# A fused two-block transformer kernel on one core: the queries' RMS norm moved into the exponential's scale, the keys' sums of squares taken in two rounded parts

## The chip, the core and the metric

The kernel runs on one core of one Trainium2 chip, whatever else the chip has. The metric is device time in microseconds from start to end of the program. The core has a matrix engine (TensorE, PE in the profile, with its weight loads as PEld), a vector engine (VectorE, DVE), an activation engine (ScalarE, ACT), a general engine (GpSimd, POOL) and a queue engine (SyncE, SP) that issues the DMAs.

## The reference, cut to what matters

The first block (attention with compressed, selected and window branches, retention, a gated feed-forward part) is not touched. The second block has two layers; each projects the tokens, and its attention normalizes queries and keys before a softmax:

```python
q1 = rms_norm_2(q[..., 0, :], q_norm_g[i])      # over the 64 numbers of a half head
q2 = rms_norm_2(q[..., 1, :], q_norm_g[i])
k1 = rms_norm_2(k[..., 0, :], k_norm_g[i])
k2 = rms_norm_2(k[..., 1, :], k_norm_g[i])
def rms_norm_2(x, g):
    y = xf * lax.rsqrt(jnp.mean(xf * xf, axis=-1, keepdims=True) + EPS)
    return (y * g).astype(x.dtype)
s = einsum('bhqd,bhkd->bhqk', q, k) * 64 ** -0.5
att = softmax(mask(s1)) - lam * softmax(mask(s2))
```

There are 512 tokens, 4 heads of two halves of 64 numbers, and 2 such layers.

## The kernel before, in words

All activations lie turned: 128 features over the partitions, 512 tokens along the free dimension. Weights come in as a stream of units of 128x1024 numbers. For each unit ScalarE rounds the raw numbers to a high part (`hi_part`, called by `ahead`, line 396), GpSimd takes the rest in four quarters (`lo_part`, line 339), and TensorE makes 8 times three products of 512 columns in the one-pass type F32R: high by high, high by low, low by high (`product`, lines 745 to 747). A unit is 24 matmuls. The order of each engine's work is written out by hand; semaphores with running counts tie the engines together. The two-part operands of the tokens are `a_hi`, `a_lo` and `y_hi`, `y_lo`.

A layer of the second block begins with four units for the values, then eight units (`L_QK`) that give in turn the queries and the keys of a head: unit j even is the queries of head j/2, j odd the keys. While TensorE runs unit j, the other engines finish unit j-1:

- VectorE, `qk_in(j-1)`: multiplies the PSUM bank by the tokens' norm (`scaled`, line 1220), squares the result (line 1768) and tells TensorE.
- TensorE, ahead of the fourth of the 8 triples of unit j (`k == 3`): `square_sum` (line 780), a full fp32 matmul of 512 columns with `ones2`, a block matrix of ones that sums over each half head and leaves the sum on all its 64 rows.
- ScalarE, `ahead` first, then `tile_root` (lines 411 and 419): the square root of the 128x512 sums.
- VectorE one unit later, `qk_out(j-2)`: the reciprocal of 128x512 numbers (line 1774), and the product of tile, gain and reciprocal into `qn` or `kn` (line 1777).

Then come 16 mixing slots (`L_MIX`), of one unit each. The last two tiles of queries and keys are finished in slots 0 and 1. Between the slots lie the first 8 of the 16 attention steps of the layer, one for each head and each 128 queries: scores (line 1078), mask and maximum (`maxima`, lines 1394 to 1408), exponential with a bias per row and a constant scale (`softmax_step`, line 511), the division (`step_probs`, lines 1808 to 1813), transposes at `k == 5` of the odd slots (line 1090), and the product with the values (line 1102). Slots 2 to 5 also hold a matmul of the pooled tiles (line 1136) at `k == 6`; VectorE's `pooled_out` (1823, 1826) and `mix` (1842 to 1855) run beside them.

Of the kernel before, what the change touches and what calls it, by code (L numbers as in the profile page):

```python
# [24 lines left out]
F32R = mybir.dt.float32r  # L25
# [4 lines left out]
P = 128  # L30
# [113 lines left out]
def build(nc, stream, xT, tab, decay, rope, par1, par2, pT, out):  # L144
    ctx = ExitStack()
    with ctx:
        def sb(name, shape, dt=F32):
            return ctx.enter_context(nc.sbuf_tensor(name, shape, dt))

        def sem(name):  # L150
            return ctx.enter_context(nc.semaphore(name))
# [32 lines left out]
        mix_gain = sb("mix_gain", [P, LAYERS * KD])  # L184
        work = sb("work", [P, 9 * S + 288])

        ident = cst[:, K_ID:K_ID + P]
# [3 lines left out]
        tile_a, tile_b, tile_d = ta[:, 16:], tb[:, 16:], td[:, 16:]  # L191
        eps = small[:, 60:61]
        decay_t = h[:, 0:4, :]
        rope_cn, rope_sn, rope_cr, rope_sr = (h[:, 4 + i, :] for i in range(4))
# [34 lines left out]
        merge_bank = [b_r0, b_r1, bank[0], bank[1]]  # L229

        first_unit_landed = sem("first_unit_landed")
        landed = [sem("block_landed_0"), sem("block_landed_1")]
# [152 lines left out]
        def _(act):  # L385
# [156 lines left out]
            for t in range(RH):  # L542
                u0 = t * RET_UNITS + U_RET
                for j in range(RET_UNITS):
# [3 lines left out]
                                  (prob[:, 0, 0:n], b_s0[:, 0:n], 1),  # L548
                                  (prob[:, 1, 0:n], b_s1[:, 0:n], 2)], DH ** -0.5)
                    if j == 4 or j == 0 and t > 0:  # L550
# [83 lines left out]
            for layer in range(LAYERS):  # L634
# [12 lines left out]
                def attention_step(s):  # L647
                    n = (s % QT + 1) * P
                    softmax_step([(prob[:, e, 0:n], (b_s0, b_s1)[e][:, 0:n], e) for e in range(2)],
                                 64 ** -0.5)  # L650
# [18 lines left out]
                for k in range(16):  # L669
                    if k > 0 and k % 2 == 0:  # L670
                        attention_step(k // 2)
                    ahead(ul + L_MIX, k)
                    if k == 0:
                        tile_root(tile_c, b_r1[:, :], 1.0 / 64)
# [52 lines left out]
        def _(pe):  # L727
# [68 lines left out]
            def bank4(j):  # L796
                return bank[(j + 2) % 4][:, :]
# [261 lines left out]
            for layer in range(LAYERS):  # L1059
# [48 lines left out]
                for j in range(8):  # L1108
                    unit(ul + L_QK, j, 4, [bank4(j)], a_op(), 8,
                         lambda k, j=j: square_sum((b_r0, b_r1)[(j - 1) % 2], ones2, (tile_b, tile_c)[(j - 1) % 2])  # L1110
                         if k == 3 and j > 0 else None)
# [12 lines left out]
                def mixed(slot, k):  # L1124
# [6 lines left out]
                    if k == 3 and slot == 0:  # L1131
                        square_sum(b_r1, ones2, tile_c)
                    if k == 6 and 2 <= slot <= 5:
# [56 lines left out]
        def _(dve):  # L1190
# [90 lines left out]
            V.memset(ptc, 0.0).then_inc(vector_step, steps.up())  # L1281
            V.wait_ge(vector_step, steps.now())
            V.memset(eps_squared, EPS * EPS).then_inc(vector_step, steps.up())
            V.memset(eps, EPS).then_inc(to_activate, pre.up())
# [23 lines left out]

            V.wait_ge(constants_landed, 32)
            V.wait_ge(parameters_landed, 16)  # L1310

# [75 lines left out]

            def maxima(i, mask, scale, cmp=0):

# [13 lines left out]
                if cmp:  # L1403
# [3 lines left out]
                b = 2 + cmp  # L1407
                V.tensor_scalar(small[:, 0:b], small[:, 8:8 + b], -scale, None, ALU.mult)\
                    .then_inc(max_ready, mx.up())
                V.wait_ge(max_ready, mx.now())  # L1410
# [315 lines left out]
            for layer in range(LAYERS):  # L1726
# [35 lines left out]

                value, square = (tile_a, tile_d), (tile_b, tile_c)

                def qk_in(j):
                    x, sq = value[j % 2], square[j % 2]
                    scaled(x, bank4(j), ul + L_QK, j)
                    V.tensor_tensor(sq, x, x, ALU.mult).then_inc(squares_ready, sums.up())
                    V.wait_ge(squares_ready, sums.now())

                def qk_out(j):
                    x, root_tile = value[j % 2], square[j % 2]
                    V.wait_ge(root_ready, root.due())
                    V.reciprocal(root_tile, root_tile).then_inc(vector_step, steps.up())
                    V.wait_ge(vector_step, steps.now())
                    gq = (C2_QG, C2_KG)[j % 2]
                    ins = V.scalar_tensor_tensor(out=(qn, kn)[j % 2][:, j // 2, :], in0=x,
                                                 scalar=par[:, gq:gq + 1], in1=root_tile,
                                                 op0=ALU.mult, op1=ALU.mult)
                    if j % 2:  # L1780
                        ins.then_inc(retention_input_ready, rin.up())
                        V.wait_ge(retention_input_ready, rin.now())
                    else:
                        ins.then_inc(vector_step, steps.up())

# [16 lines left out]
                def step_maxima(s):  # L1802
                    maxima(s % QT, chunk, 64 ** -0.5)

# [447 lines left out]
```

## Time and profile before

| | |
|---|---|
| Runs of the kernel | 2649.3, 2649.35, 2649.73 us (median 2649.35) |
| The profiled execution's own time | 2649.99 us |
| Its span in the profile | 2648.2 us |
| TensorE busy | 2599.5 us, 98% |
| VectorE, ScalarE, GpSimd busy | 1576.3, 849.6, 1526.7 us (60%, 32%, 58%) |
| Chain that ended last, TensorE's share | 88% |

A row of a group tells how many instructions it has, their busy time and the mean of one. A row of the timeline gives start and length in us, the engine, the line of the kernel, output and inputs, and in brackets how long the engine was idle before it and who ended that. Two matmul rows overlap, since a matmul's record runs to its drained end: what it costs in a stream is the distance between the starts.

### The profile page before, as it was taken

How to read it: one execution, taken by the hardware profiler on the slowest of the kernel's cores; microseconds unless marked ns; L12 is line 12 of the kernel's file. 1: busy time of each engine (PE TensorE's matmuls, PEld its weight loads, DVE VectorE, ACT ScalarE, POOL GpSimd, SP SyncE). 2: the span in 40 equal slices, each digit the busy share in tenths (PEclk: the TensorE clock that was granted, in tenths of full speed). 3: DMA queues.
4: the chain of work that ended last, by engine and by line, in shares of the span. 5: the costliest groups of instructions: out<-in, count | busy, mean ns of one | idle time of the engine just before them, and what ended most of it. 6: DMA issues, size and time to landing. Idle time of an engine off the chain costs nothing.

```text
span 2648.2 us, 33256 instructions
## 1 busy us (share of the span) xinstructions
PE 2599.5 (98%) x11819; PEld 2086.0 (79%) x11819; DVE 1576.3 (60%) x2192; ACT 849.6 (32%) x1245; POOL 1526.7 (58%) x1820
## 2 busy tenths in 40 slices
PE   8999999999999998999999999999899999999999
PEld 6777777888888876777888888887677788888887
DVE  6666774388483767855575432657774448443275
ACT  5444444223222332354322111133235532111122
POOL 6634345566666753554666655764355456665576
PEclk9999999999999999999999999999999999999999
DMA  5311112222223221222223222232122222222223
GB/s 188 125 49 51 62 55 105 97 95 96 96 94 107 99 102 64 80 83 92 104 80 112 96 95 95 95 111 89 62 80 96 80 104 86 105 96 95 95 95 127
DMA packets 36832, 247.47 MB, mean 93 GB/s; under 512 B 4464, under 2 KB 4848, under 8 KB 7792
## 3 DMA queue, kind: packets, MB, share of 16 engines
q1 hardware_dynamic: 34704, 238.57, 25.5%
q10 hardware_dynamic: 2016, 7.35, 0.8%
q8 instruction: 77, 1.26, 0.2%
q14 instruction: 35, 0.29, 0.0%
HBM read 243.81 MB, written 2.10 MB: 93 GB/s over the span
## 4 chain that ended last, share of the span: by engine, by line
PE 88%; DVE 7%; ACT 1%; issue 1%; DVEq 0%; ACTq 0%
PE bank L745 18%; PE bank L747 18%; PE bank L746 18%; PE both L745 9%; PE both L747 9%; PE both L746 9%; PE bank L780 1%; PE bank L1102 1%; PE both L1078 1%; PE both L930 1%; PE bank L916 1%; DVE small L1401 0%; PE bank L954 0%; PE bank L1090 0%; PE bank L1136 0%
## 5 line engine op out<-in xcount | busy, mean ns | idle before, releaser
L339 POOL TENSOR_TENSOR w_lo<-raw,w_hi 128x256 fp32r<-128x256 f32 x1784 | 1504.5, 875 | 1031.0 <-ACT w_hi L396 1030.5
L396 ACT ACTIVATE w_hi<-raw 128x1024 fp32r<-128x1024 f32 x446 | 468.9, 1057 | 993.4 <-PE bank L747 495.1
L745 PE MATMUL bank<-a_hi,w_hi 128*128 128x512 f32 x1544 | 635.3, 411 | 0.0
L747 PE MATMUL bank<-a_hi,w_lo 128*128 128x512 f32 x1544 | 605.4, 392 | 0.0
L746 PE MATMUL bank<-a_lo,w_hi 128*128 128x512 f32 x1544 | 605.1, 392 | 0.0
L745 PEld LDWEIGHTS bank<-a_hi,w_hi 128*128 128x128 f32 x1544 | 292.2, 189 | 70.5 <-issue 13.2
L746 PEld LDWEIGHTS bank<-a_lo,w_hi 128*128 128x128 f32 x1544 | 292.5, 189 | 64.2 <-issue 8.8
L747 PEld LDWEIGHTS bank<-a_hi,w_lo 128*128 128x128 f32 x1544 | 291.7, 189 | 62.7
L745 PE MATMUL bank<-y_hi,w_hi 128*128 128x512 f32 x696 | 272.7, 392 | 0.0
L747 PE MATMUL bank<-y_hi,w_lo 128*128 128x512 f32 x696 | 271.2, 390 | 0.0
L746 PE MATMUL bank<-y_lo,w_hi 128*128 128x512 f32 x696 | 271.2, 390 | 0.0
L745 PE MATMUL both<-a_hi,w_hi 128*128 128x512 f32 x656 | 260.7, 397 | 3.3 <-POOL w_lo L339 2.5
L747 PE MATMUL both<-a_hi,w_lo 128*128 128x512 f32 x656 | 256.5, 391 | 0.0
L746 PE MATMUL both<-a_lo,w_hi 128*128 128x512 f32 x656 | 256.2, 390 | 0.0
L745 PE MATMUL both<-y_hi,w_hi 128*128 128x512 f32 x504 | 197.7, 392 | 3.7 <-DVE y_lo L1492 1.8
L746 PE MATMUL both<-y_lo,w_hi 128*128 128x512 f32 x504 | 197.0, 391 | 0.0
L747 PE MATMUL both<-y_hi,w_lo 128*128 128x512 f32 x504 | 196.9, 391 | 0.0
L746 PEld LDWEIGHTS bank<-y_lo,w_hi 128*128 128x128 f32 x696 | 130.8, 188 | 27.3 <-issue 0.5
L745 PEld LDWEIGHTS bank<-y_hi,w_hi 128*128 128x128 f32 x696 | 130.8, 188 | 27.2 <-issue 0.5
L747 PEld LDWEIGHTS bank<-y_hi,w_lo 128*128 128x128 f32 x696 | 130.7, 188 | 27.2
L745 PEld LDWEIGHTS both<-a_hi,w_hi 128*128 128x128 f32 x656 | 123.6, 188 | 32.3 <-issue 2.8
L746 PEld LDWEIGHTS both<-a_lo,w_hi 128*128 128x128 f32 x656 | 123.7, 189 | 27.3 <-issue 2.1
(302 smaller groups left out, 3048.0 us busy)
## 6 DMA issues: line engine op xcount, KB each, us to landing
raw<-stream SPq DMA_DIRECT2D x223, 1024.0 KB, 4.8
h<-xT SPq DMA_DIRECT2D x8, 256.0 KB, 6.3
h<-xT ACTq DMA_DIRECT2D x1, 2048.0 KB, 7.8
outT<-h SPq DMA_DIRECT2D x8, 256.0 KB, 2.6
h<-decay ACTq DMA_DIRECT2D x1, 1024.0 KB, 5.2
h<-rope ACTq DMA_DIRECT2D x1, 1024.0 KB, 8.6
prob<-pT ACTq DMA_DIRECT2D x2, 512.0 KB, 4.4
par<-par ACTq DMA_DIRECT2D x2, 408.0 KB, 3.1
```

Source lines behind the costliest of these rows:

```text
L339: pool.tensor_tensor(w_lo[:, s, part], raw[:, s, part], w_hi[:, s, part], ALU.subtract).then_inc(lo_done, 1)
L396: act.activation(w_hi[:, s, cols], raw[:, s, cols], ACT.Copy).then_inc(hi_done, 1)
L745: pe.matmul(dst, w_hi[:, s, cols], rhs_hi(k), start=start and k == 0, stop=False)
L746: pe.matmul(dst, w_hi[:, s, cols], rhs_lo(k), start=False, stop=False)
L747: ins = pe.matmul(dst, w_lo[:, s, cols], rhs_hi(k), start=False, stop=stop and k == nk - 1)
L780: pe.matmul((b_r1 if dst is None else dst)[:, :], ones if w is None else w, ssum[:, :] if src is None else src, start=True, stop=True)\
L916: ins = pe.matmul(dst[:, a * P:S], rv[:, a, e * P:(e + 1) * P], rp[:, at:at + n], start=a == 0, stop=a == QT - 1, skip_group_check=True)
L930: ins = pe.matmul(dst[:, 0:n], (q_turned if half != g else qt)[at, cols], k_sw[g][at, 0:n], start=True, stop=True)
L1078: ins = pe.matmul(dst[:, 0:n], qn[rows, hd, i * P:(i + 1) * P], kn[rows, hd, 0:n], start=True, stop=True)
L1102: ins = pe.matmul(b_o[:, i * P:(i + 1) * P], vn[:, hd, a, :], pt[:, 0, a * P:(a + 1) * P], start=a == 0, stop=a == i, skip_group_check=True)
```

## The change

Queries: the scaled tile is written straight to `qn`, without norm and gain. ScalarE squares it into `tile_b`. TensorE sums the squares by token rather than by feature: four fp32 matmuls in which 128x128 of the squares are the stationary operand and two columns of `ones2` move, so that the 512x2 sums lie as 128x8, with tokens over the partitions. Square root and reciprocal work on 128x8 (`query_root`), with scale 1 and the constant 64 EPS, which takes the factor 1/8 of the scores in. `query_root` is then the scale, a number per row, of the exponential, and a factor of the maxima.

Keys: VectorE's square goes to `tile_a`; ScalarE squares the same tile rounded to F32R into `key_parts[0]`; VectorE subtracts it from its own square into `key_parts[1]`; TensorE sums the two with two F32R matmuls of `ones2_r` and 512 columns. Root, reciprocal and product stay on 128x512. The keys' gain becomes the product of both gains (`key_gain`).

```diff
+        ones2_r = sb("ones2_r", [P, P], F32R)
+        query_root = sb("query_root", [P, 4 * QT * 2])
+        key_parts = [y_hi[:, 8, :], y_lo[:, 8, :]]
...
-            def softmax_step(parts, last_scale):
+            def softmax_step(parts, scales):
                 act.wait_ge(max_ready, mx.due())
-                for n, (dst, src, b) in enumerate(parts):
-                    ins = act.activation(dst, src, ACT.Exp, bias=small[:, b:b + 1], scale=last_scale,
+                for (dst, src, b), scale in zip(parts, scales):
+                    ins = act.activation(dst, src, ACT.Exp, bias=small[:, b:b + 1], scale=scale,
...
+                def qk_root(j):
+                    act.wait_ge(evac, ul + (L_QK + j + 5))
+                    hd = j // 2
+                    if j % 2 == 0:
+                        act.activation(tile_b, qn[:, hd, :], ACT.Square).then_inc(query_squares_ready, 1)
+                        tile_root(query_root[:, 8 * hd:8 * hd + 8], b_r0[:, 0:8], 1.0, floor=query_floor)
+                    else:
+                        act.activation(key_parts[0], tile_d, ACT.Square).then_inc(key_hi_ready, 1)
+                        tile_root(tile_c, b_r1[:, :], 1.0 / 64)
                 for j in range(8):
                     ahead(ul + L_QK, j)
                     if j > 0:
-                        tile_root((tile_b, tile_c)[(j - 1) % 2], (b_r0, b_r1)[(j - 1) % 2][:, :], 1.0 / 64)
+                        qk_root(j - 1)
...
+            def query_sum(layer, hd):
+                pe.wait_ge(query_squares_ready, layer * 4 + hd + 1)
+                for i in range(QT):
+                    ins = pe.matmul(b_r0[:, 2 * i:2 * i + 2], tile_b[:, i * P:(i + 1) * P], ones2[:, 0:P:64],
+                                    start=True, stop=True, skip_group_check=True)
+                ins.then_inc(square_sum_done, sump.up())
+
+            def key_sum():
+                pe.wait_ge(squares_ready, sums.due())
+                pe.matmul(b_r1[:, :], ones2_r[:, :], key_parts[0], start=True, stop=False)
+                pe.matmul(b_r1[:, :], ones2_r[:, :], key_parts[1], start=False, stop=True)\
+                    .then_inc(square_sum_done, sump.up())
...
+            V.tensor_copy(ones2_r[:, :], ones2).then_inc(vector_step, steps.up())
...
+                    ins = V.scalar_tensor_tensor(out=small[:, 0:b], in0=small[:, 8:8 + b], scalar=-scale, in1=root,
+                                                 op0=ALU.mult, op1=ALU.mult)
...
+                V.tensor_tensor(key_gain, par[:, C2_QG:C2_QG + 1], par[:, C2_KG:C2_KG + 1], ALU.mult)\
+                    .then_inc(vector_step, steps.up())
                 def qk_in(j):
-                    x, sq = value[j % 2], square[j % 2]
-                    scaled(x, bank4(j), ul + L_QK, j)
-                    V.tensor_tensor(sq, x, x, ALU.mult).then_inc(squares_ready, sums.up())
+                    if j % 2 == 0:
+                        scaled(qn[:, j // 2, :], bank4(j), ul + L_QK, j)
+                        return
+                    scaled(tile_d, bank4(j), ul + L_QK, j)
+                    V.tensor_tensor(tile_a, tile_d, tile_d, ALU.mult).then_inc(vector_step, steps.up())
+                    V.wait_ge(vector_step, steps.now())
+                    V.wait_ge(key_hi_ready, layer * 4 + j // 2 + 1)
+                    V.tensor_tensor(key_parts[1], tile_a, key_parts[0], ALU.subtract)\
+                        .then_inc(squares_ready, sums.up())
                     V.wait_ge(squares_ready, sums.now())
                 def qk_out(j):
-                    x, root_tile = value[j % 2], square[j % 2]
                     V.wait_ge(root_ready, root.due())
-                    V.reciprocal(root_tile, root_tile).then_inc(vector_step, steps.up())
+                    if j % 2 == 0:
+                        r = query_root[:, 4 * j:4 * j + 8]
+                        V.reciprocal(r, r).then_inc(vector_step, steps.up())
+                        return
+                    V.reciprocal(tile_c, tile_c).then_inc(vector_step, steps.up())
                     V.wait_ge(vector_step, steps.now())
...
+                    V.scalar_tensor_tensor(out=kn[:, j // 2, :], in0=tile_d, scalar=key_gain, in1=tile_c,
+                                           op0=ALU.mult, op1=ALU.mult).then_inc(retention_input_ready, rin.up())
```

## Rows read from the trace of the kernel before

**Rows 1.** The page: busy time by engine, and the granted clock in 40 slices.
```profile
PE 2599.5 (98%) x11819; PEld 2086.0 (79%) x11819; DVE 1576.3 (60%) x2192; ACT 849.6 (32%) x1245; POOL 1526.7 (58%) x1820
PEclk9999999999999999999999999999999999999999
```

**Rows 2.** All waits of TensorE longer than 2 us: total, times, longest.
```profile
PE bank L1090 <- DVE prob L1813: 15.4, 4, 5.0
PE both L816 <- DVE a_lo L1293: 8.6, 1, 8.6
PE both L937 <- DVE prob L1450: 6.1, 7, 1.3
PE bank L927 <- DVE td L1420: 3.0, 1, 3.0
PE both L745 <- POOL w_lo L339: 2.5, 1, 2.5
```

**Rows 3.** Timeline of TensorE around the sum of head 1's query squares, layer 0.
```profile
971.87 0.39 PE L747 MATMUL bank<-a_hi,w_lo 128*128 128x512 f32 x1
972.09 1.02 PE L780 MATMUL bank<-tb,cst 128*128 128x512 f32 x2
972.55 0.79 PE L745 MATMUL bank<-a_hi,w_hi 128*128 128x512 f32 x1
973.18 0.39 PE L746 MATMUL bank<-a_lo,w_hi 128*128 128x512 f32 x1
```

**Rows 4.** Timeline of TensorE: four fp32 matmuls of 31 moving columns.
```profile
87.71 0.39 PE L747 MATMUL bank<-a_hi,w_lo 128*128 128x512 f32 x1
88.02 0.32 PEld L864 LDWEIGHTS bank<-work,par 128*64 128x64 f32 x8 [0.35 <-issue]
88.39 0.33 PE L843 MATMUL bank<-w_hi,y_hi 128*62 128x256 f32 x1
88.56 0.28 PE L844 MATMUL bank<-w_hi,y_lo 128*62 128x256 f32 x1
```

**Rows 5.** Instructions of line 864, the same loads: min/median/max of one in ns.
```profile
L864 PEld LDWEIGHTS bank<-work,par x8: 132/138/139, 88.0 to 88.2; 128*64 128x64 f32 x8
```

**Rows 6.** Chain of waits: eight transposes of 128x128 between two units.
```profile
955.72 0.88 PE bank L803 x8
```

**Rows 7.** Timeline of layer 0, unit 2 of the eight: TensorE, ScalarE, VectorE, GpSimd.
```profile
962.82 0.39 PE L745 MATMUL bank<-a_hi,w_hi 128*128 128x512 f32 x1
...
964.86 1.02 PE L780 MATMUL bank<-tile_c,cst 128*128 128x512 f32 x2
...
963.02 1.06 ACT L396 ACTIVATE w_hi<-raw 128x1024 fp32r<-128x1024 f32 x1 [2.76 <-PE both L747]
963.99 0.18 ACT L411 ACTIVATE small<-small 128x1 f32<-128x1 f32 x1
...
963.09 0.69 DVE L1220 TENSOR_TENSOR td<-both,rstd 128x512 f32<-128x512 f32 x1 [4.50 <-PE both L747]
963.82 0.69 DVE L1768 TENSOR_TENSOR tile_c<-td 128x512 f32<-128x512 f32 x1
...
964.16 3.02 POOL L339 TENSOR_TENSOR w_lo<-raw,w_hi 128x256 fp32r<-128x256 f32 x4 [4.21 <-ACT w_hi L396]
```

**Rows 8.** Instructions of line 424, ScalarE's squares: min/median/max of one in ns.
```profile
L424 ACT ACTIVATE m<-h x16: 613/616/619, 13.7 to 1793.7; 128x512 f32<-128x512 f32 x16
L424 ACT ACTIVATE m<-h,small x8: 707/707/711, 907.5 to 929.3; 128x512 f32<-128x512 f32 x8
```

**Rows 9.** Instructions of lines 1226 and 1774, VectorE: min/median/max of one in ns.
```profile
L1226 DVE TENSOR_TENSOR y_lo<-ta,y_hi x72: 692/1108/1115, 1108.3 to 2545.3; 128x512 fp32r<-128x512 f32 x72
L1774 DVE RECIPROCAL tb<-tb x8: 3352/3353/3354, 964.5 to 1863.3; 128x512 f32<-128x512 f32 x8
```

**Rows 10.** Timeline of slot 0, layer 0: VectorE, ScalarE, TensorE.
```profile
1002.05 0.69 DVE L1220 TENSOR_TENSOR td<-bank,rstd 128x512 f32<-128x512 f32 x1 [0.78 <-PE bank L747]
1002.92 0.18 ACT L411 ACTIVATE small<-small 128x1 f32<-128x1 f32 x1
1004.44 0.59 PE L780 MATMUL bank<-tile_c,cst 128*128 128x512 f32 x1
```

**Rows 11.** Timeline of VectorE and TensorE in slot 3, layer 0.
```profile
1022.19 1.24 DVE L1842 TENSOR_TENSOR tb<-ta 128x512 f32<-128x512 f32 x1
...
1027.69 0.48 DVE L1813 SCALAR_TENSOR_TENSOR prob<-prob,small 128x256 f32<-128x256 f32 x1
...
1028.23 0.44 PE L1090 MATMUL bank<-cst,prob 128*128 128x128 f32 x2 [2.93 <-DVE prob L1813]
```

**Rows 12.** Stages: busy us of PE, PEld, DVE, ACT, POOL, then granted clock.
```profile
955.70:1008.70 53.00, 53.00 (x229) 40.91 (x227) 43.24 (x37) 18.30 (x31) 24.09 (x32) 1.00 0.25 86
1030.50:1034.00 3.50, 3.50 (x12) 1.94 (x10) 3.09 (x5) 0.00 (x0) 0.00 (x0) 0.63 0.00 0
1050.00:1054.00 4.00, 4.00 (x9) 2.46 (x9) 0.89 (x2) 0.49 (x1) 0.00 (x0) 0.55 0.00 0
```

More of the change, by code:

```diff
@@ L192, in build @@
         eps = small[:, 60:61]
+        query_floor, key_gain = small[:, 62:63], small[:, 22:23]
         decay_t = h[:, 0:4, :]
@@ L229, in build @@
         merge_bank = [b_r0, b_r1, bank[0], bank[1]]
+        key_parts = [y_hi[:, 8, :], y_lo[:, 8, :]]
+        query_squares_ready = sem("query_squares_ready")
+        key_hi_ready = sem("key_hi_ready")
         first_unit_landed = sem("first_unit_landed")
@@ L548, in _ @@
                                   (prob[:, 0, 0:n], b_s0[:, 0:n], 1),
-                                  (prob[:, 1, 0:n], b_s1[:, 0:n], 2)], DH ** -0.5)
+                                  (prob[:, 1, 0:n], b_s1[:, 0:n], 2)], [DH ** -0.5] * 3)
                     if j == 4 or j == 0 and t > 0:
@@ L649, in attention_step @@
                     softmax_step([(prob[:, e, 0:n], (b_s0, b_s1)[e][:, 0:n], e) for e in range(2)],
-                                 64 ** -0.5)
+                                 [query_root[:, 2 * s + e:2 * s + e + 1] for e in range(2)])
                 def attention_copy(s):
@@ L673, in _ @@
                     if k == 0:
-                        tile_root(tile_c, b_r1[:, :], 1.0 / 64)
+                        qk_root(7)
                         load_table(ACT.Exp)
@@ L1108, in _, with qk_sum @@
                 for j in range(8):
-                    unit(ul + L_QK, j, 4, [bank4(j)], a_op(), 8,
-                         lambda k, j=j: square_sum((b_r0, b_r1)[(j - 1) % 2], ones2, (tile_b, tile_c)[(j - 1) % 2])
-                         if k == 3 and j > 0 else None)
+                    def qk_sum(k, j=j):
+                        if k == 3 and j > 0:
+                            if j % 2:
+                                query_sum(layer, j // 2)
+                            else:
+                                key_sum()
+                    unit(ul + L_QK, j, 4, [bank4(j)], a_op(), 8, qk_sum)
                     if j == 0:
@@ L1131, in mixed @@
                     if k == 3 and slot == 0:
-                        square_sum(b_r1, ones2, tile_c)
+                        key_sum()
                     if k == 6 and 2 <= slot <= 5:
@@ L1282, in _ @@
             V.wait_ge(vector_step, steps.now())
+            V.memset(query_floor, 64 * EPS).then_inc(vector_step, steps.up())
             V.memset(eps_squared, EPS * EPS).then_inc(vector_step, steps.up())
@@ L1386, in _, with maxima @@
             V.wait_ge(activated, res.due())
-            def maxima(i, mask, scale, cmp=0):
+            def maxima(i, mask, scale, cmp=0, root=None):
                 n = (i + 1) * P
@@ L1407, in maxima @@
                 b = 2 + cmp
-                V.tensor_scalar(small[:, 0:b], small[:, 8:8 + b], -scale, None, ALU.mult)\
-                    .then_inc(max_ready, mx.up())
+                if root is None:
+                    ins = V.tensor_scalar(small[:, 0:b], small[:, 8:8 + b], -scale, None, ALU.mult)
+                else:
+                    ins = V.scalar_tensor_tensor(out=small[:, 0:b], in0=small[:, 8:8 + b], scalar=-scale, in1=root,
+                                                 op0=ALU.mult, op1=ALU.mult)
+                ins.then_inc(max_ready, mx.up())
                 V.wait_ge(max_ready, mx.now())
@@ L1780, in qk_out @@
[L1780 to L1784, printed above, removed]
+                    if j % 2 == 0:
[3 more added lines that the diff above has]
+                    V.reciprocal(tile_c, tile_c).then_inc(vector_step, steps.up())
@@ L1786, in head_inverse @@
+                    V.wait_ge(vector_step, steps.now())
+                    V.scalar_tensor_tensor(out=kn[:, j // 2, :], in0=tile_d, scalar=key_gain, in1=tile_c,
+                                           op0=ALU.mult, op1=ALU.mult).then_inc(retention_input_ready, rin.up())
+                    V.wait_ge(retention_input_ready, rin.now())
                 def head_inverse(hd, c, parts=2):
@@ L1802, in step_maxima @@
                 def step_maxima(s):
-                    maxima(s % QT, chunk, 64 ** -0.5)
+                    maxima(s % QT, chunk, 1.0, root=query_root[:, 2 * s:2 * s + 2])
                 def step_probs(s):
```

5 lines of the change are left out of this document (removed).

## The prediction

> **What bounds the kernel now.** I read the page first: TensorE is busy 98% of the span at full clock in nearly every slice, the others 32 to 60% [rows 1]. So only two things can move the time: what TensorE has to run, and what makes it wait. Then TensorE's waits: 31 us in all of 2648, the largest at line 1090, and none at line 780 on the squares of queries or keys [rows 2]. The eight query and key units and slot 0 of layer 0 have TensorE busy 53.00 of 53.00 us [rows 12]. VectorE has 43.24 us of work in them and may be late by a little without any cost. Last, the timelines, since the change lengthens a chain that ends in a TensorE instruction.
>
> **TensorE, keys.** The old sum lies between L747 at 971.87 and L746 at 973.18 [rows 3]: 1.31 us, of which two ordinary matmuls take 2 x 0.227 (nine of them take 2.04 us, from 962.82 to 964.86 [rows 7]). So an fp32 sum costs 0.86 us. The new one is two F32R matmuls of the same shape as the ordinary ones, 0.45 us. Eight key sums (4 heads, 2 layers) save 8 x 0.41 = 3.2 us.
>
> **TensorE, queries.** Four fp32 matmuls with 128 stationary and 2 moving columns replace one of 0.86 us. The trace has none of that kind. Nearest are the four of line 864 with 31 moving and 64 stationary columns: the stretch from L747 at 87.71 to L844 at 88.56 [rows 4] less 0.23 for L747 and less 0.12 for a matmul of 256 columns leaves 0.50 us. The loads of its eight records take 0.32 us together, 0.138 each [rows 4, 5], so their starts are (0.32 - 0.138) / 7 = 26 ns apart, and 8 x 26 = 0.21; the other 0.29 is a start-up cost (0.35 us of issue). With 128 columns I scale 26 to 52 to 55 ns: 0.44 us for eight. From above, transposes with 128 columns both ways are 0.88 / 8 = 0.11 us apart [rows 6] with no start-up cost: 0.88 for eight, and 1.17 with the 0.29. I take 0.55, near the lower end, because the stationary is full width as in the transposes, which show no start-up cost, and because two moving columns leave only the load. Eight query sums save 8 x 0.31 = 2.5 us; bounds from +3.4 us saved (0.44) to 2.5 us lost (1.17).
>
> The Trainium skill, TensorE: Matmul & The Clock Gate, LDWEIGHTS (loading the stationary operand), gives a load as columns / 1.2 ns: by it 128 columns are 107 ns. The 26 ns that I read for 64 columns is half of the 53 ns of that rule, so the trace speaks against it. By the rule eight loads are 0.85 us and the query sums would save nothing; that is rival B below, priced there from the transposes.
>
> **The new wait, keys.** This is what the change puts on the path. Count from the start U of the unit (962.82 [rows 7]). The sum is due at U + 2.04. Before, VectorE's square ended at 963.82 + 0.69 = U + 1.69, in time. Now ScalarE does its rounding first (from U + 0.20, next instruction at 963.99, U + 1.17), then the square: 0.62 us as at line 424 without a tile as scale [rows 8], to U + 1.79. VectorE, which has its own square by then, starts the subtraction at about U + 1.83. Subtractions of this form take 0.69 to 1.11 us, median 1.11 [rows 9]; GpSimd starts its four quarters at 964.16, U + 1.34, for 3.02 us [rows 7], so they overlap this one. It ends at U + 2.52 to 2.94, and TensorE goes on 0.04 us later, plus about 0.07 for a load that is no longer ahead (line 1090 starts 0.06 after VectorE's end [rows 11]). The wait is 0.6 to 1.05 us; I take 0.9, since GpSimd is running. It stands behind nothing but the weight stream: everything queued on TensorE shifts with it.
>
> The Trainium skill, GPSIMD Engine Reference, Specifications, says that GpSimd shares its SBUF interfaces with VectorE and contends with instructions of two SBUF inputs; the two levels of line 1226 agree, and by the rule the subtraction is at the upper one.
>
> Of the four keys of a layer three meet it, 6 in all: 5.4 us. The fourth is summed in slot 0, where the scores stand before the unit: VectorE starts its tile at 1002.05 and ScalarE is free at 1002.92, with the sum due at 1004.44 [rows 10]. The same chain is done at 1002.92 + 0.62 + 0.04 + (0.69 to 1.11) + 0.04 = 1004.31 to 1004.73: 0 to 0.3 us of wait, 0.2 taken, twice, 0.4 us.
>
> **The wait, queries.** ScalarE's square ends at U + 1.79; the first load is due about 0.2 us ahead of U + 2.04. Bounds 0 to 0.2 us each; 0.05 for the four that follow no transposes, 0.2 us.
>
> **What is hidden.** VectorE loses eight reciprocals of 3.35 us [rows 9] and gains small work; it had 9.8 us of room in that stage [rows 12], so this is worth nothing by itself. ScalarE gains 16 squares of 0.62 and loses eight 512-wide roots for 8-wide ones, at 18.30 us of 53 busy [rows 12]. The exponentials get a scale per row: the rows of line 424 show 0.09 us for that [rows 8], 64 times. No wait of TensorE hangs on them but line 1090's, and there VectorE's pooled tiles end last (1022.19 to 1027.69 [rows 11]); with that cover gone they would cost 5.8 us. Line 1090's waits themselves start from a TensorE matmul in the slot before and stay. The maximum's last product takes a second tensor of two columns: 0. The copy of `ones2` at the start: 0 to 0.3, 0.2 taken.
>
> **Sum.** -3.2 - 2.5 + 5.4 + 0.4 + 0.2 + 0.2 = +0.5 us. The profiled execution took 2649.99, so 2650.5; it lies 0.64 above the median of the runs, so for the median 2649.9 us. About 0.2% (5.3 us) is what a measurement of this kernel can tell from no change.
>
> **The rivals.**
> B, the query sums cost what the transposes' distance says, 0.88 us: nothing is saved there, +3.0 instead of +0.5, 2652.4. For it: a 128-wide load never shows below 0.11 in the trace. Against it: the 26 ns at 64.
>
> C, slower: the key chain is later than I have it. It has three links on two engines, and each quarter of GpSimd may delay the subtraction at its start and in its run. The place is the sum at `k == 3` of units 2, 4 and 6. With the other terms as above, it decides from a wait of (5.3 - 0.5 + 5.4) / 6 = 1.7 us each; at 1.8 the time is 2655.3. Against it: both ends of my estimate are below 1.1. A second square in another table of ScalarE would do it too (line 424 shows no table load between other functions, so I do not expect one).
>
> D, faster: the keys' wait is 0.6 (-1.8), the query sums cost 0.44 (-0.9), and the stages behind fall better. After TensorE's waits at line 1090 it runs at half clock for some us (0.63 over 3.5 us and 0.55 over 4 [rows 12], so 1.2 of 2.4 GHz most of the time). A stretch of 3.5 us less in each layer gives 2 x 1.7 = 3.4. Together -5.6 from the median, 2643.8. For it: VectorE is a little ahead at slot 0. Against it: the wait at line 1090 follows from TensorE's own order.
>
> E, the sums do not come out cheaper at all, or something else bounds them: about 2655.
>
> **How the numbers follow.** Forecast 0.62, B 0.14, C 0.11, D 0.10, E 0.03. B and the forecast lie within 0.2%. D just passes it, C and half of E too. So faster 0.10, same 0.77, slower 0.13. The range: the bounds of the key wait (-1.8 to +0.9), of the query sums (-0.9 to +5.0) and of the clock behind (3.4 either way) do not come together; I take 2645.0 to 2654.8.
>
> **What would show it.** In the profile of the changed kernel: TensorE's waits list line of the key sum <- VectorE `y_lo`, 6 to 8 times, 0.9 each; the subtraction at about 1.1 us; the distance from the start of the last matmul ahead of the query sum to the second behind it, about 0.55 + 0.45 us (B: 0.88 + 0.45); line 1090's waits still near 15 us; no table load before the squares. Wrong if the key sum does not wait at all (then faster), or if its wait is over 1.7 us, or if a new wait shows in steps 0 to 7 of the attention.

## The result, and the profile after

The changed kernel takes 2653.82 us (median of 22 runs, 2651.91 to 2655.2) against 2649.73 for the kernel before (22 runs, 2646.79 to 2651.56): a ratio of 1.0015, 95% interval 1.0008 to 1.0021. It is 0.15% slower, inside what the prediction called no change and inside its range, but 3.9 us above its time, on the side of its slower rivals. The profiled execution has a span of 2652.4 us, 4.2 more. One of the eleven runs of a kernel below (the queries' squares in F32R) fell in a slower state, 2957.65 us at a mean granted clock of 0.826, and is left out of its median.

The page: TensorE has 1.3 us less to do, VectorE 28.9 less, ScalarE 10.9 more [rows 1]. TensorE has less work and the kernel is longer, so it waits.

```profile
span 2652.4 us, 33372 instructions
PE 2598.2 (98%) x11867; PEld 2087.3 (79%) x11867; DVE 1547.4 (58%) x2188; ACT 860.5 (32%) x1261; POOL 1529.5 (58%) x1820
```

TensorE's waits after: total, times, longest. Against [rows 2] the line of the key sum (L812, on the subtraction L1817) is new, and so is a small one on ScalarE's square of a query tile (L667). The transposes' wait grew from 15.4 to 16.4.

```profile
PE bank L1122 <- DVE prob L1860: 16.4, 4, 5.5
...
PE bank L812 <- DVE y_lo L1817: 4.2, 6, 0.7
...
PE bank L805 <- ACT tb L667: 0.3, 1, 0.3
```

The stage of the eight units in layer 0, with the same columns as [rows 12]. TensorE, busy for the whole of that stage before, has 2.2 of 55 us idle:

```profile
955.50:1010.50 55.00, 52.82 (x254) 42.71 (x253) 29.00 (x33) 20.52 (x38) 25.94 (x34) 1.00 0.24 78
```

**A key sum, layer 0, timeline of all engines after** (the counterpart of [rows 7]; the unit starts at U = 963.48):

```profile
963.48 0.39 PE L762 MATMUL bank<-a_hi,w_hi 128*128 128x512 f32 x1
...
965.29 0.39 PE L764 MATMUL bank<-a_hi,w_lo 128*128 128x512 f32 x1
966.37 0.50 PE L812 MATMUL bank<-y_hi,ones_r 128*128 128x512 f32 x1 [0.69 <-DVE y_lo L1817]
966.71 0.39 PE L813 MATMUL bank<-y_lo,ones_r 128*128 128x512 f32 x1
966.94 0.39 PE L762 MATMUL bank<-a_hi,w_hi 128*128 128x512 f32 x1
...
963.68 1.06 ACT L402 ACTIVATE w_hi<-raw 128x1024 fp32r<-128x1024 f32 x1 [3.30 <-PE both L764]
964.65 0.61 ACT L670 ACTIVATE y_hi<-td 128x512 fp32r<-128x512 f32 x1
...
964.47 0.69 DVE L1814 TENSOR_TENSOR ta<-td 128x512 f32<-128x512 f32 x1
965.36 0.95 DVE L1817 TENSOR_TENSOR y_lo<-ta,y_hi 128x512 fp32r<-128x512 f32 x1 [0.20 <-ACT y_hi L670]
...
964.82 3.47 POOL L345 TENSOR_TENSOR w_lo<-raw,w_hi 128x256 fp32r<-128x256 f32 x4 [4.39 <-ACT w_hi L402]
```

ScalarE rounds the weights, then squares; VectorE waits 0.20 us for it and subtracts, beside GpSimd, in 0.95 us; TensorE goes on 0.06 us after its end. Without a sum L762 would follow L764 at 965.52; it comes at 966.94. A key sum costs 1.42 us, of which 2 x 0.227 is work, 0.85 lateness (966.37 less 965.52) and 0.11 a restart: the first matmul's load is not ahead of it. The old one cost 0.86. The five others of this kind cost 1.41 to 1.46, and all eight subtractions take 0.95 to 0.98 us.

**A query sum, timelines of TensorE and of its loads after** (the counterpart of [rows 3]):

```profile
973.07 0.40 PE L764 MATMUL bank<-a_hi,w_lo 128*128 128x512 f32 x1
973.30 0.95 PE L805 MATMUL bank<-cst,tb 128*128 128x2 f32 x8
974.11 0.48 PE L762 MATMUL bank<-a_hi,w_hi 128*128 128x512 f32 x1
974.43 0.40 PE L763 MATMUL bank<-a_lo,w_hi 128*128 128x512 f32 x1
...
973.07 1.09 PEld L805 LDWEIGHTS bank<-cst,tb 128*128 128x128 f32 x8
```

From L764 to L763 it is 1.36 us, less two matmuls 0.91. The eight loads take 1.09 us, the last about 0.19 long, so the last starts at 973.97. The first starts 0.23 us ahead of its matmul, under the ordinary one; the other seven are (973.97 - 973.30) / 6 = 0.11 apart, as 0.91 / 8 = 0.11 says too. Two columns move, and the sum costs 0.05 more than the old one with 512 did.

**Where the 4.2 us come from.** Starts of the same weight matmul in both traces, after less before: +0.6 ahead of the eight sums of layer 0; +2.37 after them; +3.20 ahead of those of layer 1; +5.52 after them; +4.2 at the end. The steps across the eight sums: six keys +0.54 to +0.59 each, the two of slot 0 -0.05 each, seven queries 0.00 to +0.05, and the first query of layer 1 +0.63. So keys +3.3, queries +0.8, the start +0.6, and the rest (slots 1 to 15 and behind) -0.5.

Of the +0.6, 0.38 is the copy of the ones, which stands ahead of the first `scaled` on VectorE. The time from the 24th to the 25th of the weight matmuls (`product`) is 0.37 to 0.39 us longer than before in every kernel with the copy there, and at most 0.02 longer in the four without it. The other 0.2 is within the scatter of single traces, which start these matmuls between 0.45 us earlier and 1.09 us later than the kernel before.

```profile
30.33 0.51 DVE L1348 CAST ones_r<-cst 128x128 fp32r<-128x128 f32 x1
30.93 0.69 DVE L1257 TENSOR_TENSOR tile_c<-both,rstd 128x512 f32<-128x512 f32 x1
```

The first query of layer 1: ScalarE's rounding of the weights waited 6 us for a weight block that landed late, and the square stood behind it. Before, it waited there too, with nothing that TensorE needed behind it.

```profile
1819.05 1.06 ACT L402 ACTIVATE w_hi<-raw 128x1024 fp32r<-128x1024 f32 x1 [6.06 <-DMA raw<-stream]
1820.01 0.61 ACT L667 ACTIVATE tb<-work 128x512 f32<-128x512 f32 x1
...
1820.68 1.05 PE L805 MATMUL bank<-cst,tb 128*128 128x2 f32 x8 [0.33 <-ACT tb L667]
```

### The profile page after: what moved, and what is told of

It reads as the page before. It is cut to its first block, busy times and chain, and to the rows that moved or that the text cites. A ratio compares the mean times of both kernels' runs of the same rounds, so it can differ in the third digit from the quotient of the medians.

```text
span 2652.4 us, 33372 instructions
## 1 busy us (share of the span) xinstructions
PE 2598.2 (98%) x11867; PEld 2087.3 (79%) x11867; DVE 1547.4 (58%) x2188; ACT 860.5 (32%) x1261; POOL 1529.5 (58%) x1820
## 4 chain that ended last, share of the span: by engine, by line
PE 30%; POOL 29%; issue 23%; DVE 1%; POOLq 0%; ACT 0%; DMA 0%; DVEq 0%; SPq 0%
POOL w_lo L345 29%; PE bank L762 6%; PE bank L764 6%; PE bank L763 6%; PE both L762 3%; PE both L763 3%; PE both L764 3%; PE bank L1134 0%; PE both L1110 0%; PE bank L797 0%; ACT w_hi L402 0%; PE bank L1122 0%; DMA raw<-stream 0%; POOLq L383 0%; POOLq L342 0%
## 5 line engine op out<-in xcount | busy, mean ns | idle before, releaser
L762 PE MATMUL bank<-a_hi,w_hi 128*128 128x512 f32 x1544 | 630.3, 408 | 0.0
L764 PE MATMUL bank<-a_hi,w_lo 128*128 128x512 f32 x1544 | 604.5, 392 | 0.0
L763 PE MATMUL bank<-a_lo,w_hi 128*128 128x512 f32 x1544 | 604.2, 391 | 0.0
L762 PEld LDWEIGHTS bank<-a_hi,w_hi 128*128 128x128 f32 x1544 | 291.8, 189 | 68.6 <-issue 10.8
L763 PEld LDWEIGHTS bank<-a_lo,w_hi 128*128 128x128 f32 x1544 | 292.0, 189 | 62.0 <-issue 6.2
L764 PEld LDWEIGHTS bank<-a_hi,w_lo 128*128 128x128 f32 x1544 | 291.2, 189 | 62.9
L762 PE MATMUL bank<-y_hi,w_hi 128*128 128x512 f32 x696 | 272.4, 391 | 0.0
L764 PE MATMUL bank<-y_hi,w_lo 128*128 128x512 f32 x696 | 271.0, 389 | 0.0
L763 PE MATMUL bank<-y_lo,w_hi 128*128 128x512 f32 x696 | 270.9, 389 | 0.0
L762 PE MATMUL both<-a_hi,w_hi 128*128 128x512 f32 x656 | 258.3, 394 | 3.3 <-POOL w_lo L345 2.5
L764 PE MATMUL both<-a_hi,w_lo 128*128 128x512 f32 x656 | 256.1, 390 | 0.0
L763 PE MATMUL both<-a_lo,w_hi 128*128 128x512 f32 x656 | 255.9, 390 | 0.0
L762 PE MATMUL both<-y_hi,w_hi 128*128 128x512 f32 x504 | 197.6, 392 | 3.7 <-DVE y_lo L1535 1.8
L763 PE MATMUL both<-y_lo,w_hi 128*128 128x512 f32 x504 | 196.8, 390 | 0.0
L764 PE MATMUL both<-y_hi,w_lo 128*128 128x512 f32 x504 | 196.7, 390 | 0.0
L763 PEld LDWEIGHTS bank<-y_lo,w_hi 128*128 128x128 f32 x696 | 130.7, 188 | 27.4 <-issue 0.5
L762 PEld LDWEIGHTS bank<-y_hi,w_hi 128*128 128x128 f32 x696 | 130.7, 188 | 27.3 <-issue 0.5
L764 PEld LDWEIGHTS bank<-y_hi,w_lo 128*128 128x128 f32 x696 | 130.6, 188 | 27.3
L762 PEld LDWEIGHTS both<-a_hi,w_hi 128*128 128x128 f32 x656 | 123.5, 188 | 31.0 <-POOL w_lo L345 2.8
L763 PEld LDWEIGHTS both<-a_lo,w_hi 128*128 128x128 f32 x656 | 123.6, 188 | 26.0 <-issue 0.7
```

What stands on the lines that cost most here:

```text
L762: pe.matmul(dst, w_hi[:, s, cols], rhs_hi(k), start=start and k == 0, stop=False)
L763: pe.matmul(dst, w_hi[:, s, cols], rhs_lo(k), start=False, stop=False)
L764: ins = pe.matmul(dst, w_lo[:, s, cols], rhs_hi(k), start=False, stop=stop and k == nk - 1)
```

## The experiments

Ten kernels, all of which compute the whole reference. A ratio is to runs of the kernel before that were taken beside the experiment; a kernel with one run has a profile but no ratio, and its time alone decides nothing.

### The key sums two triples later

```diff
-                        if k == 3 and j > 0:
-                            if j % 2:
-                                query_sum(layer, j // 2)
-                            else:
-                                key_sum()
+                        if k == 3 and j % 2:
+                            query_sum(layer, j // 2)
+                        if k == 5 and j > 0 and j % 2 == 0:
+                            key_sum()
```

> The changed kernel with one edit: the key sums of units 2, 4 and 6 stand ahead of the sixth triple of the unit instead of the fourth, 1.36 us later; the one of slot 0 stays. Theory: in the changed kernel such a sum takes 1.42 us of TensorE's line (two matmuls of 0.23 and 0.96 of lateness and restart), since the subtraction ends 0.85 us after the sum is due; later by 1.36 us it does not wait, a key costs 0.45 and six of them give 5.8 us back: 2653.8 - 5.8 = 2648.0, 0.07% below the kernel before. Rival: TensorE's position is not what is short; the later sum makes root, reciprocal and scores late and the wait comes back there or in the slots, so 2652 to 2654.

Measured: 2646.7 us (11 runs), 7.1 below the changed kernel, ratio to the kernel before 0.9991 (0.9982 to 1.0). The stage has TensorE busy 54.93 of 55 us, and its waits list has no key sum:

```profile
955.50:1010.50 55.00, 54.93 (x266) 45.29 (x266) 31.62 (x38) 22.01 (x40) 26.87 (x35) 1.00 0.28 96
```

```profile
966.26 0.40 PE L764 MATMUL bank<-a_hi,w_lo 128*128 128x512 f32 x1
966.49 0.39 PE L812 MATMUL bank<-y_hi,ones_r 128*128 128x512 f32 x1
966.73 0.39 PE L813 MATMUL bank<-y_lo,ones_r 128*128 128x512 f32 x1
966.95 0.40 PE L762 MATMUL bank<-a_hi,w_hi 128*128 128x512 f32 x1
```

From 966.26 to 966.95 there are three ordinary distances: a key sum is 0.46 us. The wait did not come back elsewhere. The rival falls. The gain is 1.3 us over the 5.8 expected. The trace shows where more can come from: in the 50 us behind slot 0 of layer 0 the granted clock is 0.97, where the changed kernel has 0.90 (last three columns: clock, DMA share, GB/s):

```profile
1010.00:1060.00 50.00, 41.95 (x166) 30.18 (x165) 36.55 (x54) 9.80 (x21) 17.26 (x20) 0.90 0.17 63
1010.00:1060.00 50.00, 41.99 (x178) 30.77 (x177) 38.78 (x56) 10.87 (x21) 18.73 (x22) 0.97 0.13 44
```

The first row is of the changed kernel, the second of this one. In layer 1 it is the other way round, 0.93 there and 0.90 here.

### The key sums one triple later

The same with `k == 4`.

> The changed kernel with the key sums of units 2, 4 and 6 one triple later (ahead of the fifth), 0.68 us. Theory: lateness plus restart was 0.96 us at the fourth, of which 0.85 is lateness; 0.17 is left and a restart, so a sum costs 0.45 + 0.2 to 0.3, and six of them are 4.1 to 4.6 us cheaper than in the changed kernel: about 2649.5. Rival, the wait is of a fixed kind (a latency of the semaphore or of the load after any wait): it stays near 0.5 or more.

Measured in one run: 2648.65 us, 5.2 below the changed kernel; the timeline is what decides. The distance from L764 (965.92) to the L762 behind the sum (966.88) is 0.96 us, less one matmul 0.73 (the others up to 0.78):

```profile
965.92 0.39 PE L764 MATMUL bank<-a_hi,w_lo 128*128 128x512 f32 x1
966.31 0.50 PE L812 MATMUL bank<-y_hi,ones_r 128*128 128x512 f32 x1
966.65 0.39 PE L813 MATMUL bank<-y_lo,ones_r 128*128 128x512 f32 x1
966.88 0.40 PE L762 MATMUL bank<-a_hi,w_hi 128*128 128x512 f32 x1
```

So the key sum costs 1.42, 0.73 and 0.46 us ahead of the fourth, fifth and sixth triple: 0.68 us of the wait go with the first triple, and the rest, with about 0.1 of restart, with the second. It is lateness, not a latency of its own.

### The keys' part alone

Queries keep the old sum (`square_sum(b_r0, ones2, tile_b)`), root, reciprocal and product, and the exponential its constant scale:

```diff
-                        act.activation(tile_b, qn[:, hd, :], ACT.Square).then_inc(query_squares_ready, 1)
-                        tile_root(query_root[:, 8 * hd:8 * hd + 8], b_r0[:, 0:8], 1.0, floor=query_floor)
+                        tile_root(tile_b, b_r0[:, :], 1.0 / 64)
...
-                                 [query_root[:, 2 * s + e:2 * s + e + 1] for e in range(2)])
+                                 [64 ** -0.5] * 2)
```

> Only the keys' part of the change; the queries have their old fp32 sum of 512 columns, root, reciprocal and product, and the exponential its constant scale. Theory: six sums at +0.56 and two at -0.41 each, +2.5, and 0.5 at the start for the copy of the ones: 2649.7 + 3.1 = 2652.8, with slots 2 to 5 as before (waits of the transposes near 15.4 us in all). Rival: the keys are harmless and the queries' part (their sum, the exponential's scale per row) carries the 4.1 us, then 2650.

Measured: 2653.74 us (11 runs, ratio 1.0016, 1.0007 to 1.0025), as slow as the whole change. The six waits are there, 4.2 us in all. The time is 0.9 above what was expected, and one part of the expectation failed: the transposes' waits did not stay near 15.4 us but are 16.3. So they grow without the exponential's scale per row too:

```profile
PE bank L1117 <- DVE prob L1861: 16.3, 4, 4.9
...
PE bank L807 <- DVE y_lo L1815: 4.2, 6, 0.7
```

### The queries' part alone

```diff
-                        act.activation(key_parts[0], tile_d, ACT.Square).then_inc(key_hi_ready, 1)
...
-                pe.matmul(b_r1[:, :], ones2_r[:, :], key_parts[0], start=True, stop=False)
-                pe.matmul(b_r1[:, :], ones2_r[:, :], key_parts[1], start=False, stop=True)\
+                square_sum(b_r1, ones2, tile_c)
```

> Only the queries' part; the keys have their old sum of 0.86 us and no copy of the ones at the start. Theory: eight query sums of four fp32 matmuls with two moving columns cost 0.90 instead of 0.86, +0.4; the first of layer 1 is late by 0.6 behind a weight block; the exponentials with a scale per row add about 0.5 a layer in slots 3 and 5: 2649.7 + 1 to 2 = 2651.2. Rival, the prediction's price (0.55 a sum): 2647.2 to 2648.5.

Measured: 2649.94 us (11 runs), ratio 1.0002 (0.9993 to 1.0011): no difference from the kernel before, and 1.3 under what was expected. The rival, the prediction's price for the query sum, asked for 2647.2 to 2648.5; the median lies above that, but the interval reaches into it, so the time alone does not rule it out; the timeline does (0.91 us a sum). The transposes' waits are 16.0. The half microsecond a layer that was expected of the scale per row is not shown either, since they are 16.3 without it.

### The queries' squares in F32R

```diff
+        query_squares = sb("query_squares", [P, S], F32R)
-                        act.activation(tile_b, qn[:, hd, :], ACT.Square).then_inc(query_squares_ready, 1)
+                        act.activation(query_squares[:, :], qn[:, hd, :], ACT.Square).then_inc(query_squares_ready, 1)
-                    ins = pe.matmul(b_r0[:, 2 * i:2 * i + 2], tile_b[:, i * P:(i + 1) * P], ones2[:, 0:P:64],
+                    ins = pe.matmul(b_r0[:, 2 * i:2 * i + 2], query_squares[:, i * P:(i + 1) * P], ones2_r[:, 0:P:64],
```

> The changed kernel, but the queries' squares are written in F32R and summed with the rounded ones, so a matmul is one pass instead of two: 4 loads and 4 matmuls of 2 columns instead of 8. Theory: the load of 128 stationary columns at about 0.107 us is the price, so a sum falls from 0.90 to about 0.45 and the kernel by 8 x 0.45 = 3.6 us, to 2650.2. Rival: the price is a fixed start-up of some 0.3 to 0.5 us, or a floor for each instruction that is not the load; then the gain is under 2 us. If the load of F32R is faster than that of fp32, the sum is under 0.3.

Measured: 2650.8 us, the median of ten runs (ratio 1.0004, 0.9994 to 1.0013), 3.1 below the changed kernel where 3.6 were expected. In the trace the sum is 0.91 - 0.45 = 0.46 us, from L765 at 972.21 to L764 at 973.12:

```profile
972.21 0.40 PE L765 MATMUL bank<-a_hi,w_lo 128*128 128x512 f32 x1
972.44 0.50 PE L806 MATMUL bank<-ones_r,query_squares 128*128 128x2 f32 x4
972.81 0.47 PE L763 MATMUL bank<-a_hi,w_hi 128*128 128x512 f32 x1
973.12 0.39 PE L764 MATMUL bank<-a_lo,w_hi 128*128 128x512 f32 x1
```

Half the records, half the price: 0.11 us each in either type, and no start-up cost to speak of. A fixed price a sum, which was one rival, and a faster load of F32R, which would have given under 0.3, are both out.

### 64 columns moving instead of 2

```diff
-                    ins = pe.matmul(b_r0[:, 2 * i:2 * i + 2], tile_b[:, i * P:(i + 1) * P], ones2[:, 0:P:64],
+                    ins = pe.matmul(b_r0[:, 64 * i:64 * i + 64], tile_b[:, i * P:(i + 1) * P], ones2[:, 0:P:2],
```

> The changed kernel, but 64 columns of the block of ones move in each of the four query matmuls instead of 2 (the same sums come out, each 32 times). Theory, the load of the 128 stationary columns (0.107 us for each of eight records) is the price: moving 64 columns in two passes is 128 / 2.4 = 53 ns and stays under it, so the stretch from the last matmul ahead to the second behind is 1.36 us as before. Rival, load and columns add up: 8 x 0.05 more, 1.75 us.

The root then reads every 32nd of the 256 sums. One run, 2654.0 us. The stretch is 972.39 to 973.75, 1.36 us as with 2 columns. The moving columns are hidden under the loads; the loads are the price. (The transposes' waits are 15.5 us in this trace.)

```profile
972.39 0.40 PE L764 MATMUL bank<-a_hi,w_lo 128*128 128x512 f32 x1
972.62 1.00 PE L805 MATMUL bank<-cst,tb 128*128 128x64 f32 x8
...
973.75 0.39 PE L763 MATMUL bank<-a_lo,w_hi 128*128 128x512 f32 x1
```

### 64 stationary columns instead of 128

```diff
-                for i in range(QT):
-                    ins = pe.matmul(b_r0[:, 2 * i:2 * i + 2], tile_b[:, i * P:(i + 1) * P], ones2[:, 0:P:64],
+                for half in range(2):
+                    for i in range(QT):
+                        at = i * P + 64 * half
+                        ins = pe.matmul(b_r0[64 * half:64 * half + 64, 2 * i:2 * i + 2], tile_b[:, at:at + 64],
+                                        ones2[:, 0:P:64], start=True, stop=True, skip_group_check=True)
```

> The changed kernel, but each query sum is eight matmuls of 64 stationary columns instead of four of 128, first all lower then all upper halves of the tokens; the same sums come out. Theory A, a load costs in proportion to its columns (53 ns for 64): 16 records are 0.85 us as before, the stretch 1.36 us. Theory B, line 864's distance of 26 ns holds for any 64 columns: 0.43 us, the stretch 0.95. Theory C, a record has a floor near 0.107: 1.7 us, the stretch 2.2.

One run, 2653.04 us. The stretch is 972.47 to 973.95, 1.48 us, nearest to theory A; less two matmuls 1.03:

```profile
972.79 0.80 PEld L807 LDWEIGHTS bank<-cst,tb 128*64 128x64 f32 x16 [0.37 <-issue]
```

The last load is 0.138 long, so 16 starts are on average (0.80 - 0.138) / 15 = 44 ns apart. The average hides a pattern, which the single loads in the trace show. They start at 972.79, .85, .90, .96, 973.02, .08, .14 and .19, and at 973.05, .11, .16, .22, .28, .34, .40 and .46: two series of eight, 55 to 59 ns from one load to the next in each, and the second begins before the first has ended. All eight sums of the kernel look like this. Eight loads are what each half of the output partitions has. While one series runs, two to three loads are under way at once, while both run, four to five (the loads in 10 ns from 972.99, 973.15 and 973.35, each row with the start of the first):

```profile
972.90 0.20 PEld L807 LDWEIGHTS bank<-cst,tb 128*64 128x64 f32 x2
973.02 0.26 PEld L807 LDWEIGHTS bank<-cst,tb 128*64 128x64 f32 x5
973.22 0.25 PEld L807 LDWEIGHTS bank<-cst,tb 128*64 128x64 f32 x3
```

So a load's cost falls with its columns, 57 ns for 64 against 112 for 128, as theory A has it, and loads for the two halves go side by side. The same reading explains line 864 in the kernel before, where each half has four loads: they start at 88.024, .079, .135 and .194, and at 88.038, .093, .149 and .207, again 55 to 59 ns apart in each series, the two series 14 ns apart. The 26 ns that the prediction scaled is the average over two series side by side, and not the price of a load of 64 columns. That the series are the halves is read from their counts and from the order in which the kernel issues them; no run has one half alone.

The remaining 0.3 us is not one start-up. About 0.10 passes between the end of the ordinary matmul's turn (972.47 + 0.23) and the first load. From the last load (973.46) to the next ordinary matmul (973.61) it is 0.10 more than from one load to the next. And 0.11 is lost between that matmul and the one behind it (973.95). The full-width sum has only the last of the three, 0.09 there.

### All sums later, and the copy moved

All sums of units 1 to 7 at `k == 5`, and:

```diff
-            V.tensor_copy(ones2_r[:, :], ones2).then_inc(vector_step, steps.up())
...
+                if layer == 0:
+                    V.tensor_copy(ones2_r[:, :], ones2).then_inc(ones_rounded, 1)
+                    V.wait_ge(ones_rounded, 1)
```

> All sums of units 1 to 7 stand ahead of the sixth triple, and the copy of the ones is made after the values' tiles of layer 0 instead of ahead of the first block. Theory: against the keys' sums alone at that place (2646.7) the start gives 0.4 back and the first query sum of layer 1, which waited behind a weight block, 0.6: 2645.7. Rival: the start's 0.4 and the late query are absorbed elsewhere, 2646.7.

Measured: 2645.83 us (11 runs), ratio 0.9987 (0.9978 to 0.9996). In the trace the first query of layer 1 costs what the others do, 0.91 us, and the 0.38 us at the start are gone. The copy itself is shorter at its new place, 0.21 us instead of 0.51 (0.21 in the next kernel too, but 0.84 in the last):

```profile
951.33 0.21 DVE L1811 CAST ones_r<-cst 128x128 fp32r<-128x128 f32 x1
```

### The same with F32R squares of the queries

> The same with the queries' squares and ones in F32R. Theory: eight sums fall from 0.90 to 0.45 us (3.6 in all), 2645.7 - 3.6 = 2642.1, 0.28% under the kernel before. Rival: the four matmuls end sooner but something of VectorE or ScalarE is then late in slots 0 to 5, 2644 to 2645.

Measured: 2642.97 us (10 runs), ratio 0.9976 (0.9966 to 0.9985). A gain of 2.9 us over the one above where 3.6 was expected; the query sums are 0.46 us each. It is faster than both kernels.

### And the weights' rounding ahead of the exponentials in slots 2 and 4

```diff
+                    if k in (2, 4):
+                        ahead(ul + L_MIX, k)
                     if k > 0 and k % 2 == 0:
                         attention_step(k // 2)
-                    ahead(ul + L_MIX, k)
+                    if k not in (2, 4):
+                        ahead(ul + L_MIX, k)
```

> The kernel with all sums later, the copy moved and F32R squares of the queries (2643.0), plus one edit: in slots 2 and 4 ScalarE rounds the weight unit ahead of the exponentials instead of behind them. Theory: its rounding then need not wait for the maxima, GpSimd starts its quarters some 1 to 2 us sooner, and fewer of VectorE's pooling steps (1.1 us beside GpSimd, 0.69 alone) run beside them; the waits of the transposes fall from 16.4 to 12 to 14 us, 2640 to 2641. Rival: GpSimd's second unit comes at its own time and lies on VectorE's chain in any case; 2643.

Measured: 2641.14 us (6 runs), ratio 0.9968 (0.9956 to 0.998), the lowest median here, 0.3% under the kernel before. Its interval and that of the kernel above it (0.9966 to 0.9985) overlap, so the times alone do not settle that this edit gains. In the trace the transposes' waits fell from 16.5 to 13.9:

```profile
PE bank L1129 <- DVE prob L1869: 13.9, 4, 4.9
```

VectorE in slot 3 shows how: its first two pooling steps run at 0.69 us where the kernel above has 1.20 and 1.11, and the kernel before 1.24 for the first [rows 11]. The first row is of the kernel above, the others are of this one:

```profile
1018.99 1.20 DVE L1895 TENSOR_TENSOR tb<-ta 128x512 f32<-128x512 f32 x1
...
1017.88 0.69 DVE L1898 TENSOR_TENSOR tb<-ta 128x512 f32<-128x512 f32 x1
1018.61 0.69 DVE L1898 TENSOR_TENSOR td<-tb 128x512 f32<-128x512 f32 x1
1019.34 1.11 DVE L1904 SCALAR_TENSOR_TENSOR tb<-td,ta 128x512 f32<-128x512 f32 x1
...
1018.83 3.58 POOL L347 TENSOR_TENSOR w_lo<-raw,w_hi 128x256 fp32r<-128x256 f32 x4 [4.52 <-ACT w_hi L404]
```

GpSimd's quarters for the slot are over before the chain begins, and only the next unit's, from 1018.83, lie on it. VectorE's steps of this slot that start before that moment take 0.69 us, the one that starts after it 1.11.

## Why the prediction was right or wrong

**What bounds the kernel.** Right. TensorE was full in the stage, and the time moved by what it had to run and what it waited for; VectorE's 28.9 us less gave nothing that the trace shows. A slip on the way: TensorE's waits are not 31 us in all, the five rows of [rows 2] alone add up to 35.6. Nothing was worked out from that.

**Keys, work.** Right: a sum that does not wait is 0.46 us (0.45 predicted), by the later positions.

**Keys, wait.** Right in mechanism, place and number of times: six, on the subtraction, beside GpSimd. The size was 0.96 to 1.00 us for lateness and restart against 0.9, inside its bounds (0.6 to 1.05; its own terms add up to 1.01 at the upper end). The subtraction took 0.95 to 0.98 us, less than the 1.11 of the upper level that the prediction took from [rows 9], and started 0.05 us later; from its end until TensorE streamed again at its pace 0.06 + 0.11 us were lost where 0.04 + 0.07 stood. The two sums in slot 0 lost 0.35 each rather than 0.2 (-0.05 measured where the work alone is -0.41). Together +0.7 us. Moving the sum settles the cause: in the trace 5.8 us come back in the sums themselves without touching anything else.

**Queries, work.** This is the term that failed. The prediction took 0.55 us a sum, near its lower end, by scaling line 864's 26 ns for 64 columns to 128. It measured 0.91, near the upper row, the transposes' 0.88. Eight sums give +0.4 where -2.5 stood: 2.9 us of the error. The step that was wrong is the reading of the 26 ns as the price of one load: it is the average of two series of loads, one for each half of the output partitions, that run side by side at 55 to 59 ns each. A full-width load covers both halves, and twice 57 ns is the 0.11 that was measured. A second row in the same list, the transposes, had the full width and the right price. The 0.29 us of start-up was rightly left out: full-width loads show none.

The rule of the Trainium skill (TensorE: Matmul & The Clock Gate, LDWEIGHTS (loading the stationary operand)), columns / 1.2 ns, gives an estimate of 0.85 us for the eight loads. This case's trace agrees with it: 0.11 us a load at 128 columns, in fp32 and in F32R, with 64 moving columns making no difference, and 55 to 59 ns at 64 columns within one series, where the rule has 53. The prediction's sentence that the trace speaks against the rule came of the same misreading of the 26 ns. Rival B, at 0.14, was what the query sums did.

**Queries, wait.** Seven were as predicted, within 0.05 us. The eighth was not seen: ScalarE's queue has the rounding of a weight unit ahead of the square, and that waits for a DMA at one place. This sum cost 0.6 us more than the others. The row was to be had: before, ScalarE's rounding waited there for the same block, 5.97 us.

```profile
1815.77 1.06 ACT L396 ACTIVATE w_hi<-raw 128x1024 fp32r<-128x1024 f32 x1 [5.97 <-DMA raw<-stream]
```

**The start.** The copy cost 0.38 us against 0.2, above its bound of 0.3: it took 0.51 us, and VectorE had no room there. Behind the values' tiles the same copy took 0.21, 0.21 and 0.84 us in three kernels, so the 0.51 is not a fixed length; what held it was not tried.

**What is hidden.** The exponential's scale costs ScalarE 0.09 us (0.56 against 0.47 for 256 columns), as predicted, and no time that shows: with the constant scale the waits of the transposes were 16.3, with it 16.4. No table load stands before the squares. Right.

**The sum.** By the trace +0.6 for the start, +3.3 for keys, +0.8 for queries, -0.5 behind: 4.2. Predicted: +0.2, +2.6, -2.3, 0. That the time fell inside the range, and that no change was the right call, is due to the width of both: 3.9 us of error fit in them, 1.0 us short of the range's upper end, and most of the error is in one term. The sum itself was not right. What lies behind the sums is TensorE's clock and the waits of the transposes. In the stretch with slots 2 to 5 of layer 1 the granted clock was 0.90 before and 0.93 after:

```profile
1876.00:1926.00 50.00, 41.62 (x171) 30.17 (x170) 38.02 (x57) 10.50 (x21) 17.26 (x20) 0.93 0.13 43
```

Why the transposes' waits are 0.6 to 1 us longer in the changed kernel, in the keys' part alone and in the queries' part alone is open, and perhaps no effect of the change: the changed kernel with 64 moving columns has 15.5, against 15.4 in the kernel before, and one trace of each kernel does not tell scatter from cause. They come from VectorE steps of 0.69 or 1.11 us beside GpSimd, and the last experiment shows that shifting GpSimd moves them, but what shifted by some tenths here was not pinned down.

## What to carry to other kernels

On a saturated engine a cheaper instruction gains nothing if its operand comes later by more than it saves: compare the moment it is due with the end of the longer chain that feeds it, and where it is late, issue it some matmuls later. The whole change was 7 us faster by that alone, of which 5.8 lie in the sums themselves. A small matmul with a wide stationary operand costs its weight load, here 0.11 us for 128 columns, and an fp32 matmul has two of them, however few columns move (2 and 64 were tried). Before scaling a distance between starts, look whether it is one stream or two side by side. Before adding a step to an engine's queue, look what the step ahead of it waits for.

## What the runs showed of the hardware that was not expected

A weight load of 128 columns cost 0.11 us in fp32 and in F32R alike, and an fp32 matmul has two of them. Loads of 64 columns followed each other at 55 to 59 ns within a half of the output partitions, and the loads of the two halves ran side by side, which gave 26 ns on average (line 864) and 44 (the experiment). A group of such loads lost about 0.2 us more at its two ends than full-width loads did. A conversion of 128x128 from fp32 to F32R on VectorE took 0.21 us in two kernels, 0.84 at the same place in a third, and 0.51 ahead of the first block; GpSimd was at work beside all of them, and why they differ is open.
